# Two latent heads weighed at once on column halves, their turns a period later, and two blocks joined into one

## The chip, the cores and the metric

The kernel runs on one core of a Trainium2 chip. The metric is the device time of one execution in microseconds (us). TensorE is called PE here (its weight loads PEld), VectorE DVE, ScalarE ACT, GpSimd POOL, and SP is the engine that issues most DMAs. Each engine runs its own list of instructions in order, and they meet on semaphores.

## The reference

It is a transformer-like stack on 1024 tokens of width 1024, in f32: a block that mixes gated linear attention with latent attention, a cross attention to 256 memory tokens, a feed-forward block, and two more mixing blocks. The change touches the latent attention and the start of the cross attention:

```python
q = to_heads(rms_norm(c_q, mla_q_a_norm[l]) @ mla_w_uq[l], MLA_HEADS)      # 8 heads, 96 wide
kv = to_heads(rms_norm(c_kv, mla_kv_a_norm[l]) @ mla_w_ukv[l], MLA_HEADS)  # keys 64 (+32 rotary), values 64
...
o_mla = from_heads(causal_block_attention(q, k, v))
h = h + jnp.concatenate([o_gla, o_mla], axis=-1) @ w_out[l]
hn = rms_norm(h, norm_xa[l])
mn = rms_norm(mem, norm_mem[l])
xq = rms_norm((hn @ xa_w_q[l]).reshape(b, s, XA_HEADS, XA_HEAD_DIM), xa_q_norm[l])
```

`causal_block_attention` takes 128 queries at a time: scores against the keys up to the diagonal, softmax, then the weighted sum of values.

## The kernel before

A linear layer is three matmuls of split f32 (`product3`, lines 193 to 195), its weights streamed by SP, split into two parts by POOL (lines 186 and 188, two buffers, so a split waits until the tile before the last has been multiplied), its sum added to `h` by DVE. A plain f32 matmul leaves two records in the trace, a transpose leaves one.

`block_mla` does the latent attention. For each of the 8 heads h and each of the 8 query tiles t there is a period, written out by hand on three engines. PE: the masked scores of the following tile (into one of two halves of `acc`); in the periods t = 0 and 1 the projection of head h + 2; `turn` of this tile's weights `pr` (transposes of 128x128 blocks, in groups of at most 4, into a ring of two PSUM banks; tile t has t + 1 blocks, 36 to a head, 12 groups); `weigh` of the group before (for each block a matmul with `pT` as the loaded operand and the values, 64 columns, as the moving one); in t = 5 and 6 also `turn_qk`, the transposes of the next head's queries and keys. DVE: the row maximum of the following tile (line 1395) and its negation, the copy of a group out of the ring for t >= 4 (line 1203), a piece of the next head's preparation. ACT: the exponent (line 1239), which also sums the rows, and the other copies out of the ring. After a head, DVE's `output` divides by the sums and writes 64 columns of `o_tok`. After the last head `turn_o` turns `o_tok` (line 1123, 32 transposes), ACT and DVE split it into `mix_hi` and `mix_lo` (`high`, `low`, 1024 columns each), and `wout(1, i)` multiplies it by the output weights, 8 tiles of 48 matmuls, while DVE and ACT normalise the memory tokens (`mem_norm`) and sum the squares of the new `h` (`squares`).

Then the block ends, which all engines wait for, and `block_cross` begins: PE sums the squares over partitions (line 314), ACT takes the root, DVE and ACT make `x_hi` and `x_lo`, the normed input, one of 8 tiles after the other (lines 279 and 284 on DVE), and PE meanwhile multiplies the keys' tiles k0 to k3 of the memory, which do not need it, and then the first query tile q0, which does. The order of tiles is k0 k1 k2 k3 q0 v0 q1 v1 q2 v2 v3 q3. SP and POOL go to k0's and k1's weights in the first block, and on in the second.

## Time and profile before

| what | us |
|---|---|
| three runs, median | 3289.29 (3280.35 to 3292.79) |
| the profiled execution | 3288.64, its span 3286.9 |
| latent heads, first scores to the last weighing | 340.1 to 597.0 |
| output projection, second half, with the last turns | 597.0 to 648.05 |
| cross attention's input normed | 662.2 to 693.0 |

The span is counted from the first instruction, and stretches below are in us from its start. Of the span, PE is busy 94%, DVE 57%, ACT 29% and POOL 25%. In rows of the timeline the columns are start, duration, engine, line, operation, output<-input, shapes, number of instructions, and in brackets how long the engine was idle before and what ended that. A duration of PE overlaps the next one's: what a group costs in a row of groups is the distance of starts.

### The profile page before, as it was taken

How to read it: one execution, taken by the hardware profiler on the slowest of the kernel's cores; microseconds unless marked ns; L12 is line 12 of the kernel's file. 1: busy time of each engine (PE TensorE's matmuls, PEld its weight loads, DVE VectorE, ACT ScalarE, POOL GpSimd, SP SyncE). 2: the span in 40 equal slices, each digit the busy share in tenths (PEclk: the TensorE clock that was granted, in tenths of full speed). 3: DMA queues.
4: the chain of work that ended last, by engine and by line, in shares of the span. 5: the costliest groups of instructions: out<-in, count | busy, mean ns of one | idle time of the engine just before them, and what ended most of it. 6: DMA issues, size and time to landing. Idle time of an engine off the chain costs nothing. (4 is left out here: it accounts for less than half of the span.)

```text
span 3286.9 us, 38717 instructions
## 1 busy us (share of the span) xinstructions
PE 3084.5 (94%) x15406; PEld 2442.3 (74%) x15406; DVE 1876.9 (57%) x2775; ACT 953.0 (29%) x1838; POOL 805.7 (25%) x478
## 2 busy tenths in 40 slices
PE   8999888888999999999899999998998999999888
PEld 6777777667788888888677777776676777777666
DVE  4334565543654154254578888888444267777773
ACT  3232444324211000001324333334212244444431
POOL 3221000151433233333223323232132221121101
PEclk9998999989999999999999999999999999999999
DMA  3012000010211111112211112122331110000021
GB/s 123 33 33 94 13 1 14 14 64 26 70 45 51 45 45 51 51 45 70 75 47 46 71 45 71 46 71 78 128 102 65 45 33 27 27 26 32 8 78 64
DMA packets 47739, 170.27 MB, mean 52 GB/s; under 512 B 5200, under 2 KB 5472, under 8 KB 46688
## 3 DMA queue, kind: packets, MB, share of 16 engines
q1 hardware_dynamic: 45856, 161.85, 14.5%
q0 software_dynamic: 1728, 6.29, 0.6%
q8 instruction: 104, 1.70, 0.2%
q14 instruction: 51, 0.42, 0.0%
HBM read 145.06 MB, written 23.07 MB: 51 GB/s over the span
## 5 line engine op out<-in xcount | busy, mean ns | idle before, releaser
L193 PE MATMUL acc<-x_hi,w_hi 128*128 128x512 f32 x2048 | 843.6, 412 | 46.8 <-POOL w_lo L188 23.4
L186 POOL CAST w_hi<-w_raw 128x1024 fp32r<-128x1024 f32 x217 | 236.7, 1091 | 2408.6 <-PE acc L195 1434.8
L194 PE MATMUL acc<-x_lo,w_hi 128*128 128x512 f32 x2048 | 820.6, 401 | 0.0
L195 PE MATMUL acc<-x_hi,w_lo 128*128 128x512 f32 x2048 | 819.9, 400 | 0.0
L188 POOL TENSOR_TENSOR w_lo<-w_raw,w_hi 128x1024 fp32r<-128x1024 f32 x217 | 544.8, 2510 | 17.3
L193 PEld LDWEIGHTS acc<-x_hi,w_hi 128*128 128x128 f32 x2048 | 391.8, 191 | 152.9 <-issue 38.8
L195 PEld LDWEIGHTS acc<-x_hi,w_lo 128*128 128x128 f32 x2048 | 391.6, 191 | 95.5
L194 PEld LDWEIGHTS acc<-x_lo,w_hi 128*128 128x128 f32 x2048 | 392.4, 192 | 90.2 <-issue 2.4
L2509 DVE SCALAR_TENSOR_TENSOR acc<-ev_upad,cols,acc 128x1024 f32<-128x1024 f32 x232 | 298.2, 1285 | 5.0
L193 PE MATMUL aux<-x_hi,w_hi 128*128 128x512 f32 x464 | 198.8, 428 | 2.2 <-POOL w_lo L188 2.2
L195 PE MATMUL aux<-x_hi,w_lo 128*128 128x512 f32 x464 | 184.3, 397 | 0.0
L194 PE MATMUL aux<-x_lo,w_hi 128*128 128x512 f32 x464 | 184.1, 397 | 0.0
L1840 DVE TENSOR_TENSOR h<-h,acc 128x1024 f32<-128x1024 f32 x32 | 39.0, 1219 | 195.4 <-PE acc L195 195.4
L1827 ACT ACTIVATE ffn_conv<-ffn_conv 128x1024 f32<-128x1024 f32 x22 | 23.4, 1062 | 425.2 <-DVE ffn_conv L1865 425.2
L193 PE MATMUL acc<-g_hi,w_hi 128*128 128x512 f32 x352 | 139.2, 396 | 0.0
L194 PE MATMUL acc<-g_lo,w_hi 128*128 128x512 f32 x352 | 139.2, 396 | 0.0
L195 PE MATMUL acc<-g_hi,w_lo 128*128 128x512 f32 x352 | 139.2, 395 | 0.0
L3075 ACT ACTIVATE diff_e<-acc,diff_st 128x256 f32<-128x256 f32 (+7 forms) x128 | 94.8, 742 | 142.8 <-DVE diff_st L3197 141.3
L3196 DVE TENSOR_REDUCE diff_st<-acc 128x1 f32<-128x256 f32 (+7 forms) x128 | 96.1, 751 | 60.1 <-PE acc L3304 60.0
L195 PEld LDWEIGHTS aux<-x_hi,w_lo 128*128 128x128 f32 x464 | 87.8, 189 | 21.4
L193 PEld LDWEIGHTS aux<-x_hi,w_hi 128*128 128x128 f32 x464 | 88.1, 190 | 17.6 <-POOL w_lo L188 3.7
L1395 DVE TENSOR_REDUCE mla_stats<-acc 128x1 f32<-128x128 f32 (+3 forms) x64 | 48.5, 757 | 87.7 <-PE acc L922 66.7
(506 smaller groups left out, 5029.4 us busy)
## 6 DMA issues: line engine op xcount, KB each, us to landing
w_raw<-in_stream SPq DMA_DIRECT2D x217, 512.0 KB, 3.4
h<-in_x SPq DMA_DIRECT2D x16, 512.0 KB, 9.8
spill_h<-h SPq DMA_DIRECT2D x8, 512.0 KB, 5.2
spill<-ev_zst SPq DMA_DIRECT2D x8, 512.0 KB, 3.0
h_even<-spill_h SPq DMA_DIRECT2D x8, 512.0 KB, 7.8
ev_zr<-spill SPq DMA_DIRECT2D x8, 512.0 KB, 3.6
spill_h<-h_even SPq DMA_DIRECT2D x8, 512.0 KB, 5.4
h<-spill_h SPq DMA_DIRECT2D x8, 512.0 KB, 4.6
```

Source lines behind the costliest of these rows:

```text
L186: pool.tensor_copy(k.w_hi[slot][:], k.w_raw[slot][:]).then_inc(k.w_split, 1)
L188: pool.tensor_tensor(k.w_lo[slot][:], k.w_raw[slot][:], k.w_hi[slot][:].bitcast(F32), ALU.subtract).then_inc(k.w_split, 1)
L193: pe.matmul(out, w_hi, x_hi, start=start, stop=False)
L194: pe.matmul(out, w_hi, x_lo, start=False, stop=False)
L195: return pe.matmul(out, w_lo, x_hi, start=False, stop=stop)
L1395: dve.tensor_reduce(st[:, 28 + t % 2, 0:1], acc[:, t % 2, 0:(t + 1) * P], AX, ALU.max).then_inc(s["row_max"], 1)
L1827: act.activation(conv[:], conv[:], ACT.Silu).then_inc(s["silued"], 1)
L1840: dve.tensor_tensor(h, h, acc[:, n % 2, :], ALU.add).then_inc(summed, 1)
L2509: ins = dve.scalar_tensor_tensor(uc[:, j, :] if c == CONF_K - 1 else U, src, w, U, ALU.mult, ALU.add)
L3075: act.activation(e[:, t % 2, m, 0:n], acc[:, m, 0:n], ACT.Exp, scale=scale, bias=stat(t, m), accum_out=stat(t, 2 + m)).then_inc(s["exped"], 1)
L3196: step(dve.tensor_reduce(stat(t, 4 + m), acc[:, m, 0:n], AX, ALU.max))
```

## The change

In heads taken in pairs, an even head's turned weights are no longer used at once but kept (`kept`, 36 blocks), and those of the odd head are weighed together with them: for each block one matmul writes PSUM partitions 0 to 63 (even head) and one partitions 64 to 127 (odd head), with the values as the loaded operand (64 columns) and the turned weights as the moving one (128 columns). The result is already turned, so `turn_o` and `output` go. The division by the row sums moves into the turn: DVE writes the inverse sums on a diagonal (`weights`), and the turn is a plain f32 matmul of `pr` with that diagonal. The turn of a tile comes one period later than before, the last block of a period is n = 64, and projections stand at t = 2 and 3. Each tile of the odd head is split by ACT (`high`) and DVE (`low`) on its own, 128 columns, and the first weighing of a tile waits until the tile before (t < 4) or the one before that (t >= 4) has been read. The cross attention's programs are called at the end of `block_mla`, with k0 ahead of the sum of squares; the memory's norm is spread so that it ends before the last addition; SP and POOL run through.

```diff
+def cross_programs(k, settled):
...
+    def on_tensor(pe):
+
+        def memory_tile(kind, j):
+            n = at_of[kind, j]
+            out = acc[:, 1, j * MEM:(j + 1) * MEM] if kind == "k" else aux[:, SEQ + j * MEM:SEQ + (j + 1) * MEM]
+            pe.wait_ge(k.w_split, n * 2 + 2)
+            for i in range(KD):
+                if kind == "k" and j == 0:
+                    settled(pe, i)
+                mm = product3(pe, out, k.w_hi[n % 2][:, i * P:(i + 1) * P], k.w_lo[n % 2][:, i * P:(i + 1) * P],
+                              k.mem_hi[:, i, :], k.mem_lo[:, i, :], i == 0, i == KD - 1)
...
+        for kind, j in XA_ORDER:
+            if kind == "q":
+                query_tile(j)
+                if j == 0:
+                    key_sum()
+            else:
+                memory_tile(kind, j)
+                if kind == "k" and j == 0:
+                    norm.on_tensor(pe)
+                if kind == "v" and j != 2:
+                    head_sum(min(j, 2))
+        turn_values()
...
+    def on_scalar(act):
+        norm.root_of(act)
+        for j in range(KD):
+            norm.high(act, j)
...
-    o_tok = k.at("mla_o", 80, [P, TT, H * MLA_V])
+    kept = k.at("mla_kept", 80, [P, TT * (TT + 1) // 2, P])
+    diag = k.at("mla_diag", 119, [P, 2, P])
...
+    vt_first = [k.at(f"mla_v{i}", 137 + 2 * i, [P, TT, MLA_V]) for i in (0, 1)]
+    vt_second = k.at("mla_v2", 131, [P, TT, MLA_V])
     pT = k.at("mla_pT", 98, [P, 2, HALF])
     w_uq = k.at("mla_w_uq", 102, [P, 2, H * MLA_QK])
...
+    def turned_out(t):
+        bank = 2 if t in (4, 6) else 3
+        return aux[:, bank * HALF:bank * HALF + P]
+
+    def read_at(n):
+        return TT * (n // TT // 2) + n % TT
+
+    def pv_count(h, i):
+        return h // 2 * NG + i + 1
...
+    MEM_AT = ((), (), (0,), (1, 2), (3, 4), (5, 6), (7,), ())
+    ca, cb = STREAM["xa_kv"][0], STREAM["xa_q"][1]
+
+    def settled(pe, q):
+
+        if q == 0:
+            pe.wait_ge(s["added"], 2 * KD)
+            pe.wait_ge(mem_norm.root, 2 * mem_norm.u + 2)
+        pe.wait_ge(mem_norm.ready[0], mem_norm.ready[1] + q + 1)
+    cross_tensor, cross_scalar, cross_vector = cross_programs(k, settled)
...
-            stream_loads(k, sp, wb, wb + 2)
+            stream_loads(k, sp, wb, cb + 2)
...
         def _(pool):
-            stream_splits(k, pool, wa + 1, wb + 1)
...
-                pe.wait_ge(s["exped"], TT * h + t + 1)
+                pe.wait_ge(s["diag"], TT * h + t + 1)
                 for j, kb in enumerate(g):
-                    mm = pe.transpose(bank(key)[:, j * P:(j + 1) * P], pr[:, t % 2, kb * P:(kb + 1) * P], k.ident)
+                    mm = pe.matmul(bank(key)[:, j * P:(j + 1) * P], pr[:, t % 2, kb * P:(kb + 1) * P], diag[:, t % 2, :], start=True, stop=True)
                 mm.then_inc(s["ring_full"], 1)
...
+                n = TT * (h // 2) + t
+                wait_used(pe, ("p", h - 1, i))
                 wait_used(pe, ("p", h, i))
                 if i == 0:
                     pe.wait_ge(s["vt_done"], h + 1)
-                    pe.wait_ge(s["o_read"], h + 1)
+                if t == 4 and g[0] == 0:
+                    pe.wait_ge(s["z_copied"], 4 * min(h + 3, H))
+                if g[0] == 0 and n:
+                    pe.wait_ge(s["m_lo"], n if t < 4 else n - 1)
+                out = turned_out(t)
                 for j, kb in enumerate(g):
-                    mm = pe.matmul(aux[:, 3 * HALF + t * MLA_V:3 * HALF + (t + 1) * MLA_V], pT[:, i % 2, j * P:(j + 1) * P],
-                                   vt[h % 2][:, kb, :], start=kb == 0, stop=kb == t)
+                    pe.matmul(out[0:MLA_V, :], values_of(h - 1)[:, kb, :], kept[:, kept_at(t, kb), :], start=kb == 0, stop=kb == t)
+                    mm = pe.matmul(out[MLA_V:P, :], values_of(h)[:, kb, :], pT[:, i % 2, j * P:(j + 1) * P], start=kb == 0, stop=kb == t)
                 mm.then_inc(s["pv_done"], 1)
...
+            def period(n):
+
+                (h, t), (hm, tm) = divmod(n, TT), divmod(n - 1, TT)
+                more, ahead, i = h + 1 < H, h + 2 < H and t in (2, 3), FIRST_GROUP[tm]
+                if n + 1 < TT * H:
+                    scores(*divmod(n + 1, TT))
+                if ahead:
+                    project(h + 2, 2 * t - 4)
+                if n:
+                    turn(hm, i)
+                    if hm % 2 and i:
+                        weigh(hm, i - 1)
+                    if hm and hm % 2 == 0 and i == 0:
+                        weigh(hm - 1, NG - 1)
+                if ahead:
+                    project(h + 2, 2 * t - 3)
                 if more and t in (5, 6):
                     turn_qk("qk"[t - 5], h + 1, 0)
-                if not nxt:
-                    turn_o(0)
-                    turn_o(1)
-                if t >= 4:
-                    turn(h, i + 1)
-                    weigh(h, i)
+                if n and tm >= 4:
+                    turn(hm, i + 1)
+                    if hm % 2:
+                        weigh(hm, i)
                 if more and t in (5, 6):
                     turn_qk("qk"[t - 5], h + 1, 1)
 
-            for h in range(H):
-                for t in range(TT):
-                    period(h, t)
+            for n in range(TT * H + 1):
+                period(n)
...
             def m_ready(q):
-                if q == 3:
-                    turn_o(3)
-                pe.wait_ge(s["m_lo"], q + 1)
+                pe.wait_ge(s["m_lo"], TT * (q + 1))
...
+            cross_tensor(pe)
...
-            n = h * NG + i
-            if n >= 2:
-                eng.wait_ge(s["pv_done"], n - 1)
-            src, dst = bank(key)[:, 0:w], pT[:, i % 2, 0:w]
+            if h % 2:
+                if pv_count(h, i) > 2:
+                    eng.wait_ge(s["pv_done"], pv_count(h, i) - 2)
+                dst = pT[:, i % 2, 0:w]
+            else:
+                if h:
+                    eng.wait_ge(s["pv_done"], pv_count(h - 2, i))
+                dst = kept[:, kept_at(t, g[0]):kept_at(t, g[-1]) + 1, :].rearrange("p n c -> p (n c)")
+            src = bank(key)[:, 0:w]
...
+            def high(n):
+                p, t = divmod(n, TT)
+                act.wait_ge(s["pv_done"], p * NG + FIRST_GROUP[t + 1])
+                act.activation(m_hi[:, p, t * P:(t + 1) * P], turned_out(t), ACT.Copy).then_inc(s["m_hi"], 1)
...
-                    copy_projected(h + 2, 2 * t)
-                if t < 4:
-                    copy_turned(act, h, i)
-                if nxt:
-                    exponent(*nxt)
-                if ahead and t < 2:
-                    copy_projected(h + 2, 2 * t + 1)
+                if ahead:
+                    copy_projected(h + 2, 2 * t - 4)
+                if n and tm < 4:
+                    copy_turned(act, hm, i)
+                if ahead:
+                    copy_projected(h + 2, 2 * t - 3)
                 if more and t in (5, 6):
                     copy_qk("qk"[t - 5], h + 1, 0)
-                if not nxt:
-                    high(0)
-                    high(1)
-                if t >= 4:
-                    copy_turned(act, h, i + 1)
+                if n + 1 < TT * H:
+                    exponent(*divmod(n + 1, TT))
+                if n and tm >= 4:
+                    copy_turned(act, hm, i + 1)
                 if more and t in (5, 6):
                     copy_qk("qk"[t - 5], h + 1, 1)
-                if not more and t < 7:
+                if n >= 2 and (n - 2) // TT % 2:
+                    high(read_at(n - 2))
+                if h == H - 1 and t < 7:
                     if t == 0:
...
-                if j >= 2:
-                    mem_norm.high(act, j - 2)
-            mem_norm.high(act, KD - 2)
-            mem_norm.high(act, KD - 1)
+                for m in MEM_AT[j]:
+                    mem_norm.high(act, m)
+            cross_scalar(act)
...
+                if n >= 3 and (n - 3) // TT % 2:
+                    low(read_at(n - 3))
+                if h + 1 < H and t < 6:
                     PREPARE[t](h + 1)
                 if h + 2 < H and t >= 6:
                     (q_squares, k_squares)[t - 6](h + 2)
-                if not nxt:
-                    low(0)
-                    low(1)
-                if not more and t >= 2:
+                if h == H - 1 and t >= 2:
                     mem_norm.sum(dve, t - 1)
-                if not nxt:
+                if n == TT * H - 1:
                     mem_norm.sum(dve, t)
 
-            for h in range(H):
-                for t in range(TT):
-                    period(h, t)
-            output(H - 1)
-            low(2)
-            low(3)
+            for n in range(TT * H + 1):
+                period(n)
+            low(TT * H // 2 - 2)
+            low(TT * H // 2 - 1)
             for i in range(KD):
                 add(1, i)
                 if i:
                     squares.add(dve, i - 1)
                 if i == 2:
                     mem_norm.wait_root(dve)
-                if i >= 2:
-                    mem_norm.scale(dve, i - 2)
```

On PE, the order in the period t = 5 of head 1, the first odd one (`mla_p` and `mla_pT` are the weights before and behind the turn, `mla_v` values, `mla_qf` the next head's queries). Before:

```order
L922 MATMUL acc<-mask_mats 128x128
L1080 MATMUL aux<-mats,mla_p 128x128 x4
L1090 MATMUL aux<-mla_v_2065,mla_pT 128x64
L1113 MATMUL aux<-mats,mla_qf 96x128 x4
L1080 MATMUL aux<-mats,mla_p 128x128 x2
L1090 MATMUL aux<-mla_v_2065,mla_pT 128x64 x4
L1113 MATMUL aux<-mats,mla_qf 96x128 x4
```

and now:

```order
L922 MATMUL acc<-mask_mats 128x128
L1339 MATMUL aux<-mla_diag,mla_p 128x128 x4
L1356 MATMUL aux<-mla_kept,mla_v_2069 64x128
L1357 MATMUL aux<-mla_pT,mla_v_2071 64x128
...
L1381 MATMUL aux<-mats,mla_qf 96x128 x4
L1339 MATMUL aux<-mla_diag,mla_p 128x128
L1356 MATMUL aux<-mla_kept,mla_v_2069 64x128
L1357 MATMUL aux<-mla_pT,mla_v_2071 64x128
...
L1381 MATMUL aux<-mats,mla_qf 96x128 x4
```

Each "..." there is three more of the pairs above it: eight pairs of matmuls on halves in this period where 5 single ones were, and the turned tile is the one before (4 and 1 blocks, not 4 and 2). In the same period DVE had, and now has (`mla_stats` row maxima and sums, `mix_lo` the low part of the result):

```order
L1395 TENSOR_REDUCE mla_stats<-acc 128x1
L1397 TENSOR_SCALAR mla_stats<-mla_stats 128x1
L1203 COPY mla_pT<-aux 128x512
L1386 TENSOR_TENSOR mla_v_2064<-mla_z_2052,mla_stats 128x512
```

```order
L1650 TENSOR_REDUCE mla_stats<-acc 128x1
L1652 TENSOR_SCALAR mla_stats<-mla_stats 128x1
L1660 RECIPROCAL mla_stats<-mla_stats 128x1
L1662 TENSOR_SCALAR mla_diag<-mats,mla_stats 128x128
L1463 COPY mla_pT<-aux 128x512
L1668 TENSOR_TENSOR mix_lo<-aux,mix_hi 128x128
L1641 TENSOR_TENSOR mla_v_2070<-mla_z_2056,mla_stats 128x512
```

Two instructions came ahead of the copy, and `low` behind it.

On PE, between the output projection (`mix_hi`, `mix_lo`) and the cross attention (`mem_hi` the memory, `xa_sum` the squares), before:

```order
L195 MATMUL aux<-mix_hi,w_lo 128x512
L1027 UNCONDITIONAL_BRANCH
L1513 UNCONDITIONAL_BRANCH
L314 MATMUL aux<-xa_sum,mats 128x512 x2
L193 MATMUL acc<-mem_hi,w_hi 128x256
```

and now, k0 ahead and the block's end gone:

```order
L195 MATMUL aux<-mix_hi,w_lo 128x512
L193 MATMUL acc<-mem_hi,w_hi 128x256
...
L195 MATMUL acc<-mem_hi,w_lo 128x256
L314 MATMUL aux<-xa_sum,mats 128x512 x2
L193 MATMUL acc<-mem_hi,w_hi 128x256
```

## Rows read from the trace of the kernel before

**Rows 1.** PE in order of time, head 2: a transposed group, a weighed one, scores.

```profile
403.81 0.61 PE L1080 MATMUL aux<-mats,mla_p 128*128 128x128 f32 x4
404.25 1.01 PE L1090 MATMUL aux<-mla_v,mla_pT 128*128 128x64 f32 x8
405.10 0.44 PE L919 MATMUL acc<-mla_kT,mla_qT 96*128 96x128 f32 x2
```

**Rows 2.** PE in order of time, cross attention: f32 matmuls with 128 moving columns.

```profile
772.36 1.95 PE L1606 MATMUL aux<-xa_pT,xa_v 128*128 128x128 f32 x16
774.15 1.04 PE L1597 MATMUL aux<-mats,xa_p 128*128 128x128 f32 x8
```

**Rows 3.** PE in order of time, a later block that writes column halves.

```profile
1748.29 0.39 PE L2159 MATMUL aux<-ev_dec,ev_xtok 128*64 128x128 f32 x4
1748.50 0.39 PE L2161 MATMUL aux<-ev_cp,ev_state 128*64 128x128 f32 x4
1748.82 0.70 PE L2163 MATMUL aux<-ev_xde,ev_btok 128*128 128x256 f32 x2
```

**Rows 4.** Waits of 337 to 602: us in total, times, longest.

```profile
PE aux L1080 <- DVE mla_pT L1203: 12.5, 14, 0.9
...
PE aux L1090 <- DVE mla_pT L1203: 7.7, 10, 1.1
...
PE acc L921 <- ACT mla_kT L1229: 6.2, 8, 0.8
```

**Rows 5.** DVE in order of time, head 3: preparation, then the period t = 5.

```profile
443.36 0.28 DVE L1014 TENSOR_TENSOR mla_rt<-mla_qf,rope 128x128 f32<-128x128 f32 x1
...
456.90 1.09 DVE L1395 TENSOR_REDUCE mla_stats<-acc 128x1 f32<-128x896 f32 x1 [2.23 <-PE acc L922]
...
458.10 0.69 DVE L1203 COPY mla_pT<-aux 128x512 f32<-128x512 f32 x1
```

**Rows 6.** ACT in order of time, the same head, the period t = 6.

```profile
463.83 1.11 ACT L1239 ACTIVATE mla_p<-acc,mla_stats 128x1024 f32<-128x1024 f32 x1 [2.64 <-DVE mla_stats L1397]
```

**Rows 7.** Windows: length, busy PE, PEld, DVE, ACT, POOL, clock granted, DMA.

```profile
531.73:559.76 28.03, 23.41 (x168) 19.15 (x169) 18.48 (x44) 12.19 (x30) 0.00 (x0) 1.00 0.11 38
559.76:577.28 17.52, 17.52 (x75) 15.39 (x76) 5.82 (x15) 5.50 (x17) 0.00 (x0) 0.51 0.00 1
```

**Rows 8.** PE in order of time: scores of tile 5 of head 6, and of 0 and 5 of head 7.

```profile
543.00 1.30 PE L919 MATMUL acc<-mla_kT,mla_qT 96*128 96x512 f32 x4
...
559.76 0.77 PE L921 MATMUL acc<-mla_kT,mla_qT 96*128 96x128 f32 x2 [0.77 <-ACT mla_kT L1229]
...
577.28 1.30 PE L919 MATMUL acc<-mla_kT,mla_qT 96*128 96x512 f32 x4
```

**Rows 9.** PE in order of time, behind the last weighing.

```profile
597.00 1.04 PE L1123 MATMUL acc<-mats,mla_o 128*128 128x128 f32 x8
...
604.63 0.50 PE L193 MATMUL aux<-mix_hi,w_hi 128*128 128x512 f32 x1 [2.37 <-DVE mix_lo L1408]
...
608.23 0.59 PE L314 MATMUL acc<-mem_scratch,mats 128*128 128x256 f32 x2
```

**Rows 10.** PE in order of time, the cross attention's first work.

```profile
656.14 3.75 PE L314 MATMUL aux<-xa_sum,mats 128*128 128x512 f32 x4 [8.13 <-PEq L3328]
```

**Rows 11.** DVE in order of time, from the last addition to q0's input.

```profile
648.05 1.22 DVE L1318 TENSOR_TENSOR h<-h,aux 128x1024 f32<-128x1024 f32 x1 [2.51 <-PE aux L195]
...
662.17 2.48 DVE L279 SCALAR_TENSOR_TENSOR xa_scratch<-h,cols,xa_scratch 128x1024 f32<-128x1024 f32 x2 [6.96 <-ACT xa_scratch L261]
...
677.22 3.25 DVE L279 SCALAR_TENSOR_TENSOR xa_scratch<-h,cols,xa_scratch 128x1024 f32<-128x1024 f32 x1
...
682.47 3.28 DVE L279 SCALAR_TENSOR_TENSOR xa_scratch<-h,cols,xa_scratch 128x1024 f32<-128x1024 f32 x1
...
686.92 1.28 DVE L279 SCALAR_TENSOR_TENSOR xa_scratch<-h,cols,xa_scratch 128x1024 f32<-128x1024 f32 x1
...
689.38 1.28 DVE L279 SCALAR_TENSOR_TENSOR xa_scratch<-h,cols,xa_scratch 128x1024 f32<-128x1024 f32 x1
```

More of the change, by code:

```diff
@@ L1097, in project @@
                     pe.wait_ge(s["z_copied"], h * 4 + tp)
+                if h >= 4 and h % 2 == 0 and tp == 0:
+                    pe.wait_ge(s["m_lo"], TT * (h // 2 - 1) - 1)
                 for u in range(2):
@@ L1151, in _ @@
             scores(0, 0)
[L1153 to L1164 removed]
+            def period(n):
+                (h, t), (hm, tm) = divmod(n, TT), divmod(n - 1, TT)
+                more, ahead, i = h + 1 < H, h + 2 < H and t in (2, 3), FIRST_GROUP[tm]
[3 more added lines that the diff above has]
+                    project(h + 2, 2 * t - 4)
+                if n:
+                    turn(hm, i)
[5 more added lines that the diff above has]
+                    project(h + 2, 2 * t - 3)
                 if more and t in (5, 6):
                     turn_qk("qk"[t - 5], h + 1, 0)
[L1167 to L1172 removed]
+                if n and tm >= 4:
+                    turn(hm, i + 1)
+                    if hm % 2:
+                        weigh(hm, i)
                 if more and t in (5, 6):
                     turn_qk("qk"[t - 5], h + 1, 1)
[L1176 to L1178 removed]
+            for n in range(TT * H + 1):
+                period(n)
             weigh(H - 1, NG - 1)
[L1180 removed]
             def m_ready(q):
[L1183 to L1185 removed]
+                pe.wait_ge(s["m_lo"], TT * (q + 1))
             for i in range(KD):
[L1188 to L1189 removed]
                 wout(1, i, slots[i % 2], m_ready if i == 0 else None)
@@ L1284, in period @@
                         mem_norm.square(act, 7)
-            for h in range(H):
-                for t in range(TT):
-                    period(h, t)
-            high(2)
-            high(3)
+            for n in range(TT * H + 1):
+                period(n)
+            high(TT * H // 2 - 1)
             mem_norm.root_of(act)
@@ L1427, in _, with period @@
             tile_max(0, 0)
-            def period(h, t):
-                nxt, more = following(h, t), h + 1 < H
-                i = FIRST_GROUP[t]
-                if nxt:
-                    tile_max(*nxt)
-                if h and t == 0:
-                    output(h - 1)
-                if t >= 4:
-                    copy_turned(dve, h, i)
-                if more and t < 6:
+            def period(n):
+                (h, t), (hm, tm) = divmod(n, TT), divmod(n - 1, TT)
+                if n + 1 < TT * H:
+                    tile_max(*divmod(n + 1, TT))
+                if n < TT * H:
+                    weights(h, t)
+                if n and tm >= 4:
+                    copy_turned(dve, hm, FIRST_GROUP[tm])
+                if n >= 3 and (n - 3) // TT % 2:
+                    low(read_at(n - 3))
+                if h + 1 < H and t < 6:
                     PREPARE[t](h + 1)
@@ L1461, in _ @@
                     mem_norm.wait_root(dve)
-                if i >= 2:
-                    mem_norm.scale(dve, i - 2)
-                if i >= 3:
-                    mem_norm.low(dve, i - 3)
+                for m in MEM_AT[i]:
+                    mem_norm.scale(dve, m)
+                    if m:
+                        mem_norm.low(dve, m - 1)
+                if i == KD - 2:
+                    mem_norm.low(dve, KD - 1)
             squares.add(dve, KD - 1)
-            for j in range(KD - 3, KD):
-                if j >= KD - 2:
-                    mem_norm.scale(dve, j)
-                mem_norm.low(dve, j)
@@ L1708, in block_cross @@
+            cross_vector(dve)
     k.release()
```

492 lines of the change are left out of this document (218 added, 274 removed).

## The prediction

> **What bounds the kernel now.** I read the page first: PE is busy for 94% of the span, so only PE's own work and what makes PE wait can move the end. Then the waits of the latent stretch: PE stood 12.5 + 7.7 us for DVE's copies of turned weights and 6.2 us for ACT's copy of the next keys [rows 4], 26.4 us over 32 waits, that is in t = 4 to 7 of each head. Then PE's timeline for the price of each group, and DVE's in the same periods: DVE waited 2.23 us for PE's scores before its maximum [rows 5]. So neither is free throughout: PE is the bound, and where it waits the chain is scores, DVE's maximum, DVE's copy, PE. Last the end of the stretch and the block's end, where PE stands 8.13 us [rows 10].
>
> **The change part by part.** The sum is made against the profiled execution, 3288.6 us, 0.7 below the median of the three runs.
>
> *Turns.* A group of four transposes takes 0.44 us from start to start (403.81 to 404.25) [rows 1], 0.11 for a block. The new turn is an f32 matmul with 128 moving columns, two records a block; sixteen such records take 1.79 us (772.36 to 774.15) [rows 2], 0.224 a block. 8 heads x 36 blocks = 288, x 0.114: **+33**.
>
> *Weighing.* Four blocks take 0.85 us now [rows 1], 0.21 a block, 60.5 us for 288, though only 64 columns move. Two f32 matmuls on the two column halves, four records, take 0.21 us (1748.29 to 1748.50) [rows 3]. So 144 pairs cost 30.2 us: **-30**. These rows are of the very form that the change uses, 128*64 with 128 moving columns; if halves did not overlap here, nothing would be saved.
>
> *Going into and out of halves.* From 1748.50 to the next full-width matmul it is 0.32 us where the pair alone takes 0.21 [rows 3]: 0.11 for a change of shape, and I take the same for the way in. 12 groups in 4 pairs of heads are 48 visits: 96 x 0.11 = **+11**; nothing where PE waits anyway, so 5 to 11. The Trainium skill (TensorEngine Tiling (Array Packing), Key Properties) says that changing the tiling mode drains TensorE; that speaks against weighing in so many short visits, and the row agrees, with 0.11 us each. Without a cost for it the sum would be 11 us lower.
>
> *turn_o.* 32 transposes go: 32 x 0.11 = **-3.5**.
>
> *Waits in the loop.* I walk through t = 5 from the end of PE's scores. DVE takes 1.20 us from the start of its maximum to that of the copy (456.90 to 458.10), then 0.69 [rows 5]. Now a reciprocal and the diagonal stand between; nothing in the trace is quite that, and by the 128x128 instruction of 0.28 us [rows 5] and a dependent small one I take 0.4 (bounds 0.3 and 0.6). The copy ends at 2.3 us. PE in an even head has 4 turns (0.9) and `turn_qk` (0.45) to do until then: it waits 0.95 us where the weighing used to fill in, and 1.1 in t = 6. ACT's exponent may now start only when the tile before has been turned, and it stands ahead of the last copy of the keys: 1.11 us [rows 6] go onto the wait of 0.8 for the keys, 1.9 in all. In an odd head the first weighing of a tile waits for `low` of the tile before, which DVE does behind maximum, diagonal and copy: at 2.6 us in t = 5, where PE has done 0.9 (wait 1.7), and at 1.9 in t = 4 (wait 0.95); then 0.7 in t = 6 and 0.8 for the keys. Queued behind such a wait on PE are `turn_qk` and the scores, for which DVE waits. With 0.45 where DVE runs late between the heads this makes 8.6 us a pair of heads, 34 us, against 26.4. But no turn waits for its own exponent any more, and none of it happens beside the last head's keys; I take back 7. Waits: **0**, bounds -20 (the old ones go: the turn has a period of slack) and +20.
>
> *Behind the last weighing.* From 597.00, where it ends, to 608.23 the first output tile is done [rows 9]: 11.2 us for 24 matmuls and 16 transposes, with 2.37 us of waiting before 604.63. Fifteen matmuls take 3.60 us (604.63 to 608.23), 0.24 each, so 24 take 5.8. The split of the last tile, 128 columns by ACT and DVE, some 0.6 us, hides behind the first nine. Gain 5.4, of which 1.8 is already in *turn_o*: **-4**.
>
> *The block's end.* The last addition ends at 649.3 (648.05 + 1.22) [rows 11]. Then k0, 24 matmuls of half the columns, about 2.7 us, ends at 652.0, by when the squares are summed (ACT 1.05, DVE 1.2, both like the addition). The sum over partitions took 3.75 us at the low clock after 8.13 us of standing, ending at 659.9 [rows 10]; at the full clock about half, ending at 653.9. So the root, and DVE's start at 662.17 [rows 11], come 6.0 us earlier. DVE's two passes over a tile take 5.25 us (677.22 to 682.47) while POOL splits weights and 2.46 (686.92 to 689.38) when it does not [rows 11]. k1 and k2 are now split before DVE starts, which leaves three splits beside it where there were four: 2.8 us. q0 waits for the last of these tiles: **-9**, bounds -5 (the sum at the low clock, four splits) and -11. Loads run ahead of the splits and are covered by them.
>
> *The clock.* Head 7 begins with PE at the low level, 1.2 GHz: from 559.76 to 577.28 the granted clock was 0.51, in head 6 it was 1.00 [rows 7]. The same work, scores of tile 0 to those of tile 5, took 11.3 us in head 6 (531.73 to 543.00) and 17.5 in head 7 [rows 7, 8]: 6.2 us are the clock's. It fell behind head 6, the first without projections, in which PE did only transposes, short weighings and scores with four waits. Now the turns are real matmuls, twice as long, and PE has fewer gaps in the light heads. I take it that the fall goes: **-6**; the bound is 0. The Trainium skill (TensorE: Matmul & The Clock Gate, Part 4: PE-mode transpose) says that the full rate does not engage for transposes, which bears on the same side; by that rule alone the fall is gone.
>
> Sum: 33 - 30 + 11 - 3.5 + 0 - 4 - 9 - 6 = -9: 3288.6 - 9 = 3279.6, **3280 us**.
>
> **The rivals.**
> - *The clock falls all the same* (or at another place, once). For it: the waits of 1.9 us in even heads are longer than any in the loop now. Sum without the term: 3286. Chance 0.2.
> - *The slack works*: PE no longer waits for DVE's copies, since DVE is idle 2.23 us before the maximum [rows 5] and could be early by a period. For it: 20.2 of 26.4 us are this wait [rows 4]. Against it: the copy still stands behind the maximum of the same period. 3280 - 20 = 3260; with half of it, 3268. Chance 0.2.
> - *The reading of a tile becomes the bound* (the other side). `low` lies behind DVE's maximum, diagonal and copy, and weighing, `high`, `low` and the next weighing form a ring through three engines, over one bank. If each of 7 periods of an odd head waits 1.2 us more than I have, it is 4 x 7 x 1.2 = 34 us: 3314. It decides from 0.3 us a period (9 us eat the gain), and it is slower by my bound from 0.9. Chance 0.13.
> - *The changed block's end gives nothing*, because q0 waits for DVE's passes beside POOL as before: 3289. For it: POOL's splits slow DVE more than twofold now [rows 11]. Chance 0.07.
>
> The forecast itself has 0.4, with its own range of 3273 to 3286.
>
> **How the numbers follow.** About 0.5%, 16 us, is what a measurement of this kernel tells from no change; so faster means below 3273. All of the slack's case and a fifth of the forecast's lie there or near: 0.18 + 0.12 = 0.3. Slower, above 3306, is most of the ring's case and a little beside: 0.12. The same: 0.58. The range takes the slack's half and whole on one side, and the ring's smaller prices on the other: 3262 to 3302.
>
> **What would show it.** Right: turns of 0.22 us a block and pairs of 0.21 with 0.1 around each visit; PE waiting for DVE's `low` in t = 4 and 5 of odd heads and for the keys in even ones; a clock of 1.00 through head 7; the first output tile done 5.5 us behind the last weighing; DVE's first pass over `h` some 7 us behind the last addition, not 13. Wrong: halves that do not overlap (30 us more), waits for DVE of more than 50 us or of less than 15 in the stretch, or a clock that falls in several heads.

## The result

The changed kernel takes 3290.73 us (median of 20 runs, 3287.2 to 3298.66), the kernel before 3283.72 us on the same chips (20 runs, 3279.12 to 3292.79). The ratio is 1.0022, 95% interval 1.0015 to 1.0029: 0.2% slower. That is inside the 0.5% that I had called no change, and inside my range, but I had forecast 3280, a small gain, and the kernel went 7 us the other way. The changed kernel's profiled execution took 3291.23 us, its span is 3289.4.

I cut both traces at the same events: the first scores of latent attention, the end of the last weighing (between the two lies the loop over heads), the end of the last addition to `h`, the first `xa_qs`. The windows of the loop, before and after (length; busy PE, PEld, DVE, ACT, POOL; granted clock; DMA share, GB/s):

```profile
340.38:597.15 256.77, 227.41 (x1634) 193.26 (x1632) 152.69 (x343) 110.75 (x268) 0.28 (x1) 0.97 0.02 7
```

```profile
340.48:615.10 274.62, 238.04 (x1905) 195.84 (x1902) 175.52 (x487) 113.98 (x297) 0.28 (x1) 0.98 0.02 7
```

The loop grew by 17.9 us; of these PE is busy for 10.6 and stands for 7.2 (29.4 of standing before, 36.6 after). What PE stands for in this window (us in total, times, longest), against [rows 4]:

```profile
PE aux L1356 <- DVE mix_lo L1668: 13.0, 10, 1.7
PE acc L921 <- ACT mla_kT L1489: 10.1, 8, 1.8
PE aux L1339 <- DVE mla_kept L1463: 9.7, 10, 1.4
PE aux L1339 <- DVE mla_pT L1463: 1.9, 3, 0.6
PE aux L1339 <- DVE mla_diag L1662: 1.4, 3, 0.8
```

L1356 is the weighing, L1339 the turn, L921 the scores. PE waits 8.6 us less for DVE's copies (11.6 us, 20.2 before), but 13.0 us for a new producer, the low part of the tile before, and 3.9 us more for the keys.

Behind the loop the change does gain. DVE from the last addition on, which answers to [rows 11]:

```profile
660.56 1.22 DVE L1573 TENSOR_TENSOR h<-h,aux 128x1024 f32<-128x1024 f32 x1 [1.53 <-PE aux L195]
661.70 4.54 DVE L234 TENSOR_TENSOR xa_sum<-xa_sum,xa_sq 128x1024 f32<-128x1024 f32 x2
670.56 3.26 DVE L279 SCALAR_TENSOR_TENSOR xa_scratch<-h,cols,xa_scratch 128x1024 f32<-128x1024 f32 x2 [4.32 <-ACT xa_scratch L261]
...
716.53 1.28 DVE L1116 SCALAR_TENSOR_TENSOR xa_qs<-acc,cols,xa_rs 128x1024 f32<-128x1024 f32 x1 [3.91 <-ACT xa_rs L1078]
```

In the kernel before the first `xa_qs` starts at 710.30 us:

```profile
710.30 1.28 DVE L1673 SCALAR_TENSOR_TENSOR xa_qs<-acc,cols,xa_rs 128x1024 f32<-128x1024 f32 x1 [3.92 <-ACT xa_rs L1634]
```

From the last weighing to the end of the last addition it is 46.7 us (52.1 before), from there to `xa_qs` 54.8 (61.0 before). So the loop costs 17.9, the two stretches behind it give 5.4 and 6.2, and the changed kernel is 6.2 us late at `xa_qs`. At the end of the span it is 2.5 late in these two profiles. The code behind `xa_qs` is the same in both; from there to the end it took 2571.5 to 2580.0 us in the fourteen profiles of this study, in two groups: 2571.5 to 2572.9 in seven of the ten with the loop of pairs, this one among them, and 2576.6 to 2580.0 in the other seven, all four with the loop of single heads among them.

### The profile page after: what moved, and what is told of

It reads as the page before. It is cut to its first block and busy times, and to the rows that moved or that the text cites. A ratio compares the mean times of both kernels' runs of the same rounds, so it can differ in the third digit from the quotient of the medians.

```text
span 3289.4 us, 39469 instructions
## 1 busy us (share of the span) xinstructions
PE 3088.1 (94%) x15662; PEld 2437.9 (74%) x15662; DVE 1896.7 (58%) x2915; ACT 952.9 (29%) x1865; POOL 807.4 (25%) x478
## 3 DMA queue, kind: packets, MB, share of 16 engines
q1 hardware_dynamic: 45856, 161.85, 14.6%
## 5 line engine op out<-in xcount | busy, mean ns | idle before, releaser
L1339 PE MATMUL aux<-mla_diag,mla_p 128*128 128x128 f32 x576 | 87.7, 293 | 13.2 <-DVE mla_kept L1463 9.7
```

What stands on the lines that cost most here:

```text
L1339: mm = pe.matmul(bank(key)[:, j * P:(j + 1) * P], pr[:, t % 2, kb * P:(kb + 1) * P], diag[:, t % 2, :], start=True, stop=True)
```

## The experiments

All times are medians, the ratio is to the kernel before on the same chip, and "loop" is the window defined above, cut at the same events in each trace.

### Four kernels on where the 7 us are

**control** is the kernel before, once more.

> The kernel before, unchanged, profiled once more. My theory: 6 us of the forecast were taken from the fall of the clock in head 7 of one profile (531 to 584 us), and this fall is not in every execution: the times of before fall into two clusters, about 3279-3284 and 3288-3293 us, and the profiled execution was of the upper one. Then this profile either lies near 3282 us and lacks the fall in head 7 (steady heads of 32.3 us throughout), or lies near 3289 and has it. Rival: the fall in head 7 is in every execution, and the clusters come from elsewhere; then a profile near 3282 has the fall too.

3283.36 us (12 runs), ratio 0.9999 (0.9987 to 1.0011). Its loop:

```profile
338.53:587.63 249.10, 219.63 (x1634) 186.38 (x1632) 152.55 (x343) 110.92 (x268) 0.28 (x1) 1.00 0.02 7
```

249.1 us, not 256.8: PE stands as long (29.5 us), but is busy for 7.8 us less, and the granted clock is 1.00. So the fall of the clock in head 7, from which I took 6 us of gain, is a property of an execution and not of the kernel. Control is not free of falls: right behind the loop it has one that the profile of before lacks, 593 to 601 us at 0.79. Over the 35 runs of before that went with these four kernels, the 13 whose mean granted clock is 0.973 or less take 3288.6 us on average, the 22 above it 3281.1.

**join_only** keeps the loop over single heads and joins the blocks:

```
-            stream_splits(k, pool, wa + 1, wb + 1)
+            stream_splits(k, pool, wa + 1, cb + 1)
...
+            cross_tensor(pe)
```

> The loop over latent heads as before, heads one by one; only latent and cross attention are joined in one block, with the norm of the memory and the tiles of the stream as in the change. Theory (the join gives some 6 us where it is made, and most of that is lost again by the end of the kernel, the loop of pairs costs 12 to 18): first xa_qs some 6 us earlier against the last h add than before (56 instead of 62 us), and the whole 2 to 6 us faster than before, 3278 to 3281. Rival A (the join is worth nothing at the end, as the offset of the changed kernel falls again from 6.2 to 2.5 us behind the block, whatever stands ahead): within 1 us of before. Rival B (the join is what costs the 7 us of the medians, the pairs pay for themselves): 5 us or more slower than before.

3283.2 us, ratio 0.9985 (0.997 to 1.0). The profile has the fall (loop 256.8 us, clock 0.97) and the full gain of the join: 54.2 us from the last addition to `xa_qs`, where before and control have 61.0 and 60.9. The times (3268 to 3286) do not decide: the ratio leaves between nothing and 0.3%, while the median is 0.55 us above that of before (3282.65), outside the forecast of 3278 to 3281 and where rival A has it. Rival B is excluded. Against rival A speak only the profiles: this one, with the fall in head 7, took 3282.24 us, and the two of the kernel before that have the fall too took 3288.64 and 3289.46. That is 6 to 7 us less, but from one execution of the joined kernel.

**low_first** moves one call on DVE:

```
             def period(n):
                 (h, t), (hm, tm) = divmod(n, TT), divmod(n - 1, TT)
+                if n >= 3 and (n - 3) // TT % 2:
+                    low(read_at(n - 3))
                 if n + 1 < TT * H:
                     tile_max(*divmod(n + 1, TT))
...
-                if n >= 3 and (n - 3) // TT % 2:
-                    low(read_at(n - 3))
```

> The changed kernel with one order on VectorE: the low part of a turned tile of an odd head stands ahead of the maximum of the next tile instead of behind the weights. Theory (the waits are the missing 7 us: weighing for an odd head's tiles 4 and 5 waits 1.05 and 1.72 us for this low part, 8 times 2.8 us = 11 of the 35 us of waits per eight... that is 4 odd heads x 2.8 = 11 us): these two waits go, the maximum of the next tile comes 0.3 us later, which costs nothing where ScalarE is late anyway; 3279 to 3284, that is 7 to 11 us faster than the changed kernel. Rival (the waits are a symptom of the softmax chain: TensorE would wait as long for the diagonal instead): within 2 us of the changed kernel, 3289 to 3292, with the wait moved to the turn's line.

3275.84 us (12 runs), ratio 0.9979 (0.9969 to 0.9989): 7 us faster than before and, by the two ratios (0.9979 to 1.0022), 14 faster than the change. The waits of its loop:

```profile
PE acc L921 <- ACT mla_kT L1489: 10.1, 8, 1.8
PE aux L1339 <- DVE mla_kept L1463: 9.5, 9, 1.4
PE aux L1339 <- DVE mla_pT L1463: 1.9, 3, 0.6
PE aux L1339 <- DVE mla_diag L1662: 1.0, 2, 0.6
PE aux L1356 <- DVE mla_pT L1463: 0.6, 1, 0.6
```

The 13.0 us for the low part are gone and almost nothing has taken their place (0.6 us for `mla_pT`); the loop is 260.9 us instead of 274.6, and PE stands 23.8 us instead of 36.6. The rival, by which these waits only stand for another, is wrong. My theory had the cause but 7 to 11 us, since it counted only the two longest waits of each odd head.

**banks** gives the same wait a period of slack by another bank instead of an earlier producer:

```
-        bank = 2 if t in (4, 6) else 3
+        bank = 2 if t in (2, 4, 6) else 3
...
-                    pe.wait_ge(s["m_lo"], n if t < 4 else n - 1)
+                    pe.wait_ge(s["m_lo"], n if t < 2 else n - 1)
```

> The changed kernel with the turned output of tile 2 in the other bank as well (tiles 2, 4, 6 in one, the rest in the other), so that from tile 2 on a tile's weighing waits for the low part of the tile before the last, not of the last. Theory (as for the run with the low part ahead, the waits of 1.05 and 1.72 us per odd head are lost time): 7 to 11 us faster than the changed kernel, 3279 to 3284. Rival (TensorE would wait as long for the diagonal or the copy instead): within 2 us of the changed kernel, with the waits moved to the turn's line; or slower, if the projection that shares the bank in tiles 2 and 3 has to wait for the low part.

3280.45 us, ratio 0.9991 (0.9981 to 1.0). The wait for `mix_lo` falls from 13.0 to 2.2 us (3 times, up to 1.1), the loop to 264.5. By the two ratios it is 10 us faster than the change, as forecast. Two different ways of freeing the same link, the same kind of gain: the link was the cost.

### Four kernels on the price of the turn and on what is left to wait for

**low_transposed** is low_first with the transpose back on PE:

```
-                    mm = pe.matmul(bank(key)[:, j * P:(j + 1) * P], pr[:, t % 2, kb * P:(kb + 1) * P], diag[:, t % 2, :], start=True, stop=True)
+                    mm = pe.transpose(bank(key)[:, j * P:(j + 1) * P], pr[:, t % 2, kb * P:(kb + 1) * P], k.ident)
```

> The kernel with the low part ahead, and the turned weights made by a plain transpose on TensorE again; VectorE still makes the reciprocal and the diagonal, and TensorE still waits for them, but does not read them (so latent attention leaves out the softmax division). Only the price of the turn on TensorE is taken away. Theory (turns by a diagonal cost 0.235 us a block against 0.11, and TensorE is the bound of the loop): 288 x 0.125 = 36 us come off the loop's 260.9 if nothing waits instead; the waits of 24 us grow, because the 128x1024 maximum, the diagonal and the copies on VectorE are no shorter: I expect the loop at 229 to 239 us, and the kernel at 3246 to 3256. Rival (the loop is bound by the ring scores, maximum, exponent, diagonal, turn and copy, and TensorE's work is cover): the loop stays at 250 us or more, 3265 or above.

3264.99 us (ratio 0.9942, 0.9927 to 0.9956). Its loop, and below it that of low_first:

```profile
338.61:583.70 245.09, 206.65 (x1617) 159.01 (x1614) 175.82 (x487) 114.11 (x297) 0.28 (x1) 0.97 0.02 8
```

```profile
338.11:599.03 260.92, 237.11 (x1905) 195.11 (x1902) 177.18 (x487) 113.79 (x297) 0.28 (x1) 0.98 0.02 7
```

PE's busy time falls by 30.5 us, near the 36 of the price (and the clock is lower here), but it stands 14.6 longer (38.4 against 23.8): only 15.8 us come off. This lies between theory and rival for the loop; the kernel's time is at the rival's edge (3265). The turn has the price, but half of it is paid in time that PE would otherwise wait for DVE: the wait for `mla_kept` alone grows from 9.5 to 16.0 us:

```profile
PE aux L1339 <- DVE mla_kept L1463: 16.0, 11, 1.9
```

**low_no_diag** also drops the reciprocal and the diagonal:

```
-                if n < TT * H:
-                    weights(h, t)
...
-                pe.wait_ge(s["diag"], TT * h + t + 1)
+                pe.wait_ge(s["exped"], TT * h + t + 1)
```

> As the run with plain transposes, but VectorE makes neither reciprocal nor diagonal, and the turn waits for the exponent alone (the softmax division is left out of latent attention here too). Theory: the 0.4 us of VectorE stand ahead of the copy in each of 64 periods, and PE waits for that copy in tiles 4 to 6; with them gone 2 to 3 waits per head shrink by 0.4 us each: 7 to 10 us less than the run that keeps them. Rival (VectorE's two small instructions are hidden): within 2 us of it.

3246.81 us (ratio 0.9887, 0.9873 to 0.9901; the profiled execution is the slowest of the four, 3254.24), with a loop of 231.0 us, 14.1 less than low_transposed. That is more than the 7 to 10 I expected, but PE stands 28.0 us instead of 38.4, so only 10.4 of the 14.1 are waits; the other 3.7 are busy time of the same matmuls, which low_transposed did at a lower granted clock (0.97, here 0.98). Together the loop is 29.9 us shorter without the turns by a diagonal, 15.8 by what is taken from PE and 14.1 by what is taken from DVE, with this much of the clock in it. Both kernels leave out the division of the softmax, so this is not what a complete kernel could win; one that turns by transposes and divides elsewhere was not run.

**low_keys** is low_first with ScalarE's order changed in two tiles:

```
-                if n + 1 < TT * H:
+                if t not in (5, 6) and n + 1 < TT * H:
                     exponent(*divmod(n + 1, TT))
...
                     copy_qk("qk"[t - 5], h + 1, 1)
+                if t in (5, 6) and n + 1 < TT * H:
+                    exponent(*divmod(n + 1, TT))
```

> The kernel with the low part ahead, and in tiles 5 and 6 ScalarE's exponent behind the copy of the turned weights and the second copy of the next keys instead of ahead of them. Theory (in an even head TensorE's scores wait 1.76 us for this copy, because the 1.1 us exponent stands ahead of it, and the clock falls behind this wait in two or three of four even heads): the wait of 1.76 goes to 0.7, 4 us in all, and with it the 4 us that the low clock costs in the loop (two stretches at 424 to 512 us); 3268 to 3272 against 3275.8. Rival (the later exponent makes the next turn late, since its weights are what the turn reads): the wait moves to the turn's line and nothing is won, 3274 to 3278.

3269.12 us, ratio 0.9963 (0.995 to 0.9976). The wait for the keys is back at 6.2 us, exactly that of before [rows 4], and the loop at 256.0 us. One stretch of low clock is left, 432 to 440 us at 0.79, where low_first had 424 to 440 at 0.95 and 0.62, and 496 to 512 at 0.93 and 0.86.

**reordered** has low_first, banks, low_keys, and this on DVE:

```
-                if n < TT * H:
-                    weights(h, t)
                 if n and tm >= 4:
                     copy_turned(dve, hm, FIRST_GROUP[tm])
+                if n < TT * H:
+                    weights(h, t)
```

> The changed kernel with all four orders: low part ahead, tile 2 in the other bank, exponent behind the keys' copy in tiles 5 and 6, and VectorE's copy of the turned weights ahead of reciprocal and diagonal. Theory (each is a link of a chain for which TensorE waits: beside what the first and third give, the copy is 0.45 us earlier in tiles 4 to 7, for which even heads wait 1.0 and 1.13 us): waits in the loop 12 to 16 us instead of 24, loop 247 to 252 us, 3262 to 3268. Rival (the later diagonal makes the next turn late): as the run without it, 3269 to 3276.

3267.29 us, ratio 0.9949 (0.9936 to 0.9962): the fastest complete version of the study, 0.5% faster than before and, by the two ratios, 24 us faster than the change. Its loop and its waits:

```profile
341.61:592.36 250.75, 233.44 (x1905) 190.81 (x1902) 176.00 (x487) 114.76 (x297) 0.28 (x1) 1.00 0.02 8
```

```profile
PE acc L921 <- ACT mla_kT L1489: 6.2, 8, 0.8
PE aux L1339 <- DVE mla_kept L1463: 5.5, 8, 0.7
PE aux L1339 <- DVE mla_diag L1664: 3.2, 5, 0.7
PE aux L1339 <- DVE mla_pT L1463: 1.3, 3, 0.4
```

The clock is 1.00 throughout, so 233.4 us is what the pairs' loop costs PE at full clock, 13.8 more than control's 219.6. The later diagonal does appear (3.2 us instead of low_keys' 1.0), but costs less than the earlier copy gives (the wait for `mla_kept` is 5.5 us instead of 10.1).

### Four kernels on single terms

**visits** weighs both groups of a tile in one visit:

```
-                    if hm % 2 and i:
+                    if hm % 2 and i and tm < 4:
                         weigh(hm, i - 1)
...
                     if hm % 2:
+                        weigh(hm, i - 1)
                         weigh(hm, i)
```

> The reordered kernel with fewer changes between whole and halved matmuls: in tiles 4 to 7 of an odd head both groups are turned first, and both weighed in one visit, 8 visits a pair of heads instead of 12. Theory (each visit costs 0.2 us, 0.1 of which the turn ahead shows as 1.04 instead of 0.94): 16 visits fewer, 3.2 us off the loop's 250.8, and the kernel at 3263 to 3266. Rival (the weighing between the two turns is what covers the copies of VectorE and ScalarE): the waits for mla_pT and mla_kept grow by more than 3 us, and the kernel is at 3267 to 3272.

3270.66 us, ratio 0.9971 (0.9959 to 0.9983); the loop is 252.0 us. PE is busy 2.2 us less even with a short fall of the clock (552 to 560 us at 0.82), so visits do cost, but the wait for `mla_pT` grows from 1.3 to 4.6 us. What a visit costs is won, and the cover that it gave is lost: the rival. By the two ratios visits is 7 us slower than reordered, but its loop is only 1.2 us longer; in the profiles the rest lies behind `xa_qs` (2578.8 us to the end, reordered 2572.6), where the code is the same.

**one_half** removes one line:

```
-                    pe.matmul(out[0:MLA_V, :], values_of(h - 1)[:, kb, :], kept[:, kept_at(t, kb), :], start=kb == 0, stop=kb == t)
```

> The reordered kernel with only the odd head's half of each weighing; the even heads' products with the values are left out. Theory (the two halves run side by side, a pair costs 0.22 us as one alone does): the loop stays within 3 us of 250.8, a visit of four blocks still takes 0.9 to 1.0 us. Rival (the halves share time, and a pair costs twice what one does): the visit of four blocks takes 0.5 us, and the loop loses 144 x 0.11 = 16 us.

A single execution, 3264.35 us, with a loop of 250.4 (reordered: 250.8). PE in order of time, in an odd head: a turned group of four blocks, a visit of three with one half alone, scores, a turned group, a visit of four:

```profile
446.00 1.11 PE L1339 MATMUL aux<-mla_diag,mla_p 128*128 128x128 f32 x8
447.04 0.87 PE L1356 MATMUL aux<-mla_pT,mla_v 128*64 128x128 f32 x6
...
449.52 1.11 PE L1339 MATMUL aux<-mla_diag,mla_p 128*128 128x128 f32 x8
450.55 1.09 PE L1356 MATMUL aux<-mla_pT,mla_v 128*64 128x128 f32 x8
451.57 0.64 PE L1380 MATMUL aux<-mats,mla_qf 128*96 128x128 f32 x4
```

A visit of four blocks takes 1.02 us from start to start (450.55 to 451.57) with one half, as it does in the changed kernel with two (from its first record to the next instruction), and the turn ahead of it 1.03 (449.52 to 450.55). The second half is free. In the changed kernel the two stand side by side, and start 10 to 40 ns apart, here behind the wait of t = 4 in head 3:

```profile
457.93 0.29 PE L1356 MATMUL aux<-mla_kept,mla_v 128*64 128x128 f32 x1 [1.05 <-DVE mix_lo L1668]
457.94 0.32 PE L1357 MATMUL aux<-mla_pT,mla_v 128*64 128x128 f32 x1
458.06 0.27 PE L1356 MATMUL aux<-mla_kept,mla_v 128*64 128x128 f32 x1
458.10 0.27 PE L1357 MATMUL aux<-mla_pT,mla_v 128*64 128x128 f32 x1
```

**hold_split** holds one split on POOL:

```
-            stream_splits(k, pool, wa + 1, cb + 1)
+            stream_splits(k, pool, wa + 1, ca + 1)
+            pool.wait_ge(squares.summed, KD - 1)
+            stream_splits(k, pool, ca + 1, cb + 1)
```

> The reordered kernel, with POOL's split of k1 held until the squares of the stream are summed (I had forecast 9 us for the block's end and saw 6.2: the sum of the squares took 4.5 us for two additions beside this split). Theory (the sum over partitions starts 2.2 us earlier): VectorE's first pass over h starts 7.8 instead of 10.0 us behind the last addition, and first xa_qs 2 us earlier, 52.8 us behind it; kernel 3264 to 3267. Rival (the split is only put off, and slows a later pass over a tile by 2.5 us): first pass earlier, but xa_qs at 54.5 to 55.5 as before, 3266 to 3269.

3268.06 us, ratio 0.9968 (0.9955 to 0.9982), with the first pass earlier and nothing behind it:

```profile
639.03 1.22 DVE L1577 TENSOR_TENSOR h<-h,aux 128x1024 f32<-128x1024 f32 x1 [1.54 <-PE aux L195]
640.17 2.55 DVE L234 TENSOR_TENSOR xa_sum<-xa_sum,xa_sq 128x1024 f32<-128x1024 f32 x2
647.42 3.35 DVE L279 SCALAR_TENSOR_TENSOR xa_scratch<-h,cols,xa_scratch 128x1024 f32<-128x1024 f32 x1 [4.71 <-ACT xa_scratch L261]
```

The two additions take 2.55 us without the split beside them and 4.54 with it; the first pass over `h` starts 8.39 us behind the start of the last addition instead of 10.00. But `xa_qs` comes 54.1 us behind the last addition (reordered: 54.8): the split now slows a pass over a tile. This is nearly the rival's 54.5 to 55.5; of the 2 us won, 0.7 is left at `xa_qs`, and the kernel is not faster for it (the ratio of reordered is 0.9949). The Trainium skill (SBUF — State Buffer, SBUF: two separate sides) says that a VectorE operation with two inputs in SBUF and a GpSimd operation that reads SBUF lock each other out rather than share. These rows show that the two slow each other, and that what POOL's split took from DVE was only moved; they do not tell a lock from a share.

**before_again** is the kernel before, a third profile of it.

> One more look at the kernel before, for the fall of the clock in head 7. Of three profiles with its loop so far two have a fall of 6 to 8 us there and one has none. Theory (the fall comes in some executions and not in others, and sets which cluster of times a run belongs to): with it the loop takes 256.8 us and the run 3284 us or more, without it 249.1 us and under 3284. Rival: the loop takes 256.8 us and the time is under 3281, or the other way round.

3289.46 us with a loop of 256.8, and the clock at 0.82, 0.50 and 0.62 in the three stretches of 8 us from 552 on. As the theory has it. Of four profiles with the loop of single heads three have this fall and one has not; of ten with the loop of pairs none has a stretch of 8 us below 0.6 (the lowest are two of 0.62), but eight have shorter or weaker falls.

## Why the prediction was wrong

The prediction's own terms, against what the runs show. For the loop I take control (219.6 us busy at full clock, 29.5 standing) and reordered (233.4 busy at full clock) as the two that the clock does not blur.

**Work of PE: right.** I had +33 (turns), -30 (weighing), +11 (visits), and -1.7 of *turn_o* in the loop: +12.3. Measured is 233.4 - 219.6 = +13.8. In the changed kernel a turned group of four takes 0.94 us where no visit follows, 0.235 a block against my 0.224; a visit is dearer (a visit of four takes 1.02, not 0.85, and the turn ahead 0.1 more), about 0.25 in all where I had 0.22. That the halves overlap, on which 30 us rested, one_half shows. Over the whole loop, by the distances of starts without the waits, the turns take 35.3 us in control and 74.7 in reordered, the weighings 61.8 and 38.6: the two parts together are +16.2, where I had +14.

**Waits in the loop: the step that failed.** I walked through t = 4 to 6 of both heads and came to 34 us against 26.4, and then took 7 back because "no turn waits for its own exponent any more, and none of it happens beside the last head's keys". The waits came as walked: in an odd head 1.05 and 1.72 us for the low part (worked out: 0.95 and 1.7), in an even head 1.76 for the keys (1.9), 1.0 and 1.13 for the copy (0.95 and 1.1). The term was 0 and measured +7.2: PE stands 36.6 us where it stood 29.4. For the kinds of wait that I had walked through it is 36.1 us (worked out: 34), for the low part 13.0 instead of 10.6. Of the 7 us that I took back only 2.5 came: the waits for ACT's exponents and other copies, which I had not counted, fell from 3.6 to 1.1. I had no row for the allowance; the working that had rows was nearly right, and I corrected it by a feeling.

**The clock: the base was one execution.** -6 was the fall in head 7. Control shows that it is not always there, so a median has only a part of it. And the changed kernel has falls of its own: its loop has three stretches of 8 us at 0.79, each at or just behind the wait of 1.76 us for the keys, in even heads 0, 4 and 6. This is the last (the wait ends at 576.42 us):

```profile
576.00:584.00 8.00, 7.58 (x48) 7.25 (x48) 3.77 (x13) 2.49 (x9) 0.00 (x0) 0.79 0.00 0
584.00:592.00 8.00, 6.71 (x46) 4.71 (x44) 4.80 (x15) 4.43 (x15) 0.00 (x0) 1.00 0.00 0
```

That these waits bring the falls is not shown: head 2 has the same wait and no fall, and low_keys has a fall to 0.79 behind waits of 1.1 and 0.8. PE's busy time is 238.0 - 233.4 = 4.6 us more than in the kernel with the same matmuls at full clock. So against a before with the fall (7.8) the clock gave 3.2, and against one without it cost 4.6. I had this as a rival ("the clock falls all the same", 0.2) but only with the gain gone, not with a cost.

Together, against control: +13.8 work, +4.6 clock, +7.1 standing = +25.5, and the loops are 274.6 and 249.1, +25.5. Against the profiled execution that I used: +13.8 - 3.2 + 7.2 = +17.8, where I had 12.3 - 6 + 0 = +6.3.

**Behind the last weighing: right**, 5.4 us gained, as forecast. (Against control it is 7.0, since control's stretch has the fall at 593 to 601 us.)

```profile
593.00:601.00 8.00, 5.90 (x19) 4.71 (x20) 1.78 (x2) 0.91 (x2) 0.00 (x0) 0.79 0.00 0
```

**The block's end: the mechanism right, the size off.** I had -9, it was 61.0 - 54.8 = 6.2. DVE's start came 4.1 us earlier, not 6.0, because I had let the squares be summed in the time of two free additions, and POOL's split of k1 stands beside them (4.54 us for two, hold_split: 2.55). Of less contention in the eight passes 2.7 us came, of my 2.8, and between the last pass and `xa_qs` 0.5 was lost again.

Up to `xa_qs` I had -8.5 in all and the two profiles show +6.2. The 14.7 us between them are 7.2 of waits in the loop, 2.8 of clock, 2.8 at the block's end, 1.5 of work and 0.4 of rounding (behind the last weighing I had worked out 3.6 beside *turn_o*, and entered 4). The waits are half of it, and as much as the 7.0 us by which the medians differ.

**The rivals.** "The reading of a tile becomes the bound" named the right ring, and by my own condition it decided nothing: the ring cost 13.0 us, 2.4 more than I had already walked, or 0.1 us a period where it needed 0.3. It was no rival but a term, and low_first shows that it could be removed by moving one call. "The slack works" came true in part: 8.6 of the 20.2 us for DVE's copies went. It did not decide, because 13.0 us for the low part and 3.9 for the keys came in their place, and 11.6 remain, for copies that stand behind the maximum of the same period, the argument I had put against it. My base was high as well: the profile that I summed against took 3288.6 us, the median of the 20 runs is 3283.7. (And a fifth of the forecast's 0.4 is 0.08, not the 0.12 that I added for a faster kernel.)

What stays open: why the time from `xa_qs` to the end differs between profiles (also of the same kernel), and so why 6.2 us at `xa_qs` are 2.5 at the end of these two profiles, and 7.0 in the medians. The profiles show where it lies: in that stretch PE stands for 120 to 123 us in all fourteen, but is busy for 2449.6 to 2452.3 us in the group of 2571.5 to 2572.9 and for 2454.2 to 2458.0 in the other. The code is the same, so I take it to be mostly the granted clock again. I had no term for it, and whether the changed kernel's place in the shorter group is its own or luck, these profiles do not tell. I have shown that the clock's fall in the loop makes the loop of before 249.1 us in one execution and 256.8 in another, not what makes it fall in one and not in another. The Trainium skill (TensorE: Matmul & The Clock Gate, Part 1: The HAM clock gate) says that the same kernel can start with more or fewer slow matmuls from run to run; these rows show such a difference in mid-kernel.

## What to carry to other kernels

Where PE stands for a low-priority producer that another engine does behind longer work, order that engine's queue by who waits: a split of 0.28 us behind a maximum, a diagonal and a copy cost 13 us, and moving the call gave 14. Work taken from the bounding engine is a gain only where it did not cover a wait: half of what transposes saved on PE turned into standing, and merged visits gained nothing. And before a term is taken from one profile's clock, look at a second profile of the same kernel; do not correct a wait that is worked out from rows by an allowance that has none.

## What the runs showed of the hardware

- Two f32 matmuls of 128 moving columns on the two column halves take the time of one: 1.02 us for four pairs and for four single halves.
- A visit to the halves costs about 0.25 us: 0.1 shows in the full-width group ahead (1.03 or 1.04 instead of 0.94 us for four blocks), 0.15 in the visit itself (1.02 for four pairs of 0.22).
- In three of four even heads of the changed kernel a wait of PE of 1.76 us was followed by up to 8 us at a granted clock of 0.79, in the fourth it was not; the longer fall (8 to 16 us at 0.50) came in three of four executions of a loop in which no wait is over 1.1 us.
- Two additions of 128x1024 on DVE take 2.55 us alone and 4.54 beside a split on POOL, whose subtraction takes 3.39 us beside them and 2.34 alone.
